# Two-block transformer kernel: layer norm sums full width in two banks, mean taken off the tiles during the variance, scale by Ln and Exp, pilot of two tiles

## The chip, the cores and the metric

One core of one Trainium2 chip. The metric is the device time of one execution in microseconds (us). The profile is of one execution, and its times count from its first instruction. The engines are PE (TensorE; PEld is its weight load), DVE (VectorE), ACT (ScalarE), POOL (GpSimd) and SP (SyncE, which here issues the weight loads).

## The reference

Two blocks on x of shape 512 tokens x 1024 features, all in fp32. The first block ends in a layer norm, and the second, a pre-norm transformer of two layers, starts from its output:

```
o = concat(out_a, out_b) @ w_out
x = layer_norm(ALPHA * x + gate * o, ln_g, ln_b, 1e-5)      # mean, then mean of (x - mean)^2
# second block, layer 0 (MLA), layer 1 (HGRN2):
a = rms_norm(h, g0);  proj = a @ mla_w_in;  c_q, c_kv, k_r = split(proj)
q = rms_norm(c_q) @ w_uq;  kv = rms_norm(c_kv) @ w_ukv;  ... attention ...
h = h + rms_norm(m, g1);  a = rms_norm(h, g2);  h = h + rms_norm(relu(a @ w1)^2 @ w2, g3)
```

The angles of the rotary embedding (positions x inv_freq, then sine and cosine) are computed on the core too.

## The kernel before

Activations lie feature-major: eight tiles of 128 features x 512 tokens (M is the mixer's output, XH the residual, "mix_out" and "resid" in the profile). A matmul job multiplies one 128-column slice of a weight matrix by the eight tiles. To keep fp32 precision each operand is split into a high and a low fp32r part, and a job is 24 matmuls of 512 columns (high x high, high x low, low x high) into one PSUM bank. All jobs of the kernel are numbered. O0 + k are the eight of w_out, I0 + j the six of the MLA input and H0 - 1 its last one, 64 columns wide.

For each job SP loads the raw weights into one of two slots, ACT converts them to the high part (`high`, w_high, L1378), POOL subtracts to get the low part (`low`, w_low, L523), and PE waits for it. Jobs alternate between banks 0 and 1, so PE also waits until DVE has emptied a bank (the semaphores free["o"], free["mi"]). `high(c)` waits for job c - 2, as its slot must be free. Every engine's order is written out by hand: what stands ahead in an engine's queue runs first.

The stretch of the change:
- `out_tile(k)` on DVE empties job O0 + k: M[k] = bank * gate + XH[k], and frees the bank.
- The layer norm needs mean and variance over the features, that is over partitions and tiles. DVE adds the tiles into sum_sq (SQA). After four tiles (PILOT) PE sums SQA over partitions with a matrix of ones (the pilot mean, bank 2), ACT copies it to R2, and `centre(k)` on DVE subtracts it from each tile, so that the squares stay small. ACT squares the centred tiles into ln_squares (LNSQ), and DVE adds these up in sum_sq_kv (SQK).
- PE then sums SQA, SQK and tiles 6 and 7 and their squares into columns, one token per partition (`columns`, L1081). DVE and ACT make mean and 1/deviation in 4 columns, DVE spreads them on two diagonals, PE turns these into full-width banks 3 and 4 (L1096), and DVE makes M[k] * bank 3 - bank 4 for each tile.
- `pre_norm_of_mla` on ACT writes act_high (L1564) and LNSQ (L1566) from each finished tile, POOL makes act_low (L531), and PE's `two_jobs(I0)` starts tile by tile (L744).
- Then ACT squares, DVE adds (L366), PE sums (`norm_sum`, L1105), ACT takes the square root (`deviation`, L1557) and DVE its reciprocal (`inverse`, L2264), giving R1, which scales each latent (`latent(j)`). The kv latents get their own R3 the same way. `deviation` and `inverse` are used a third time ahead of the HGRN heads. In each HGRN head ACT takes Ln and then Exp of the same tile (L1840, L1842).
- The angles of the rotary embedding are made on DVE (L2198 to L2213) between out_tile(3) and out_tile(4), while ACT takes their sine behind R1.

DVE's helpers are `tt` (L1882, two tensors) and `stt` (L1885, tensor, scalar, tensor), so many of its operations have these lines.

## Time and profile before

| | |
|---|---|
| time, median of 3 runs | 1844.92 us (1842.28 to 1846.31) |
| the profiled execution: its time, its span | 1843.03 us, 1841.3 us |
| PE, DVE, ACT, POOL busy | 92%, 47%, 40%, 35% |
| the eight output jobs on PE | 437.6 to 476.3 us |
| first tile's act_high on ACT | 494.4 us |
| first matmul of the MLA input | 497.5 us |

A row of the timeline gives start, duration, engine, line, operation, output<-inputs, shape and count, and in brackets the engine's idle time before it and what ended it. Where several operations are merged the duration is from the first one's start to the last one's end. The granted clock is a share of TensorE's full speed: 1.0 is 2.4 GHz, 0.5 is 1.2 GHz.

### The profile page before, as it was taken

What the parts mean: (1) busy time and instruction counts of PE and PEld (TensorE: products, weight loads), DVE (VectorE), ACT (ScalarE), POOL (GpSimd) and SP (SyncE); (2) the same over time, 40 slices, a digit from 0 to 9 for tenths busy, and PEclk for the clock granted to TensorE, in tenths of its full rate; (3) what the DMA queues carried; (4) which work ended last, traced back from release to release, by engine and by line L of the source; (5) the groups of instructions that cost most, each with busy time, mean ns of one, the idle gap of its engine ahead of it and who ended that gap; (6) DMA issues with size and microseconds to landing.
All of it is one profiled execution on the core that took longest, in us unless ns stands there. A gap on an engine that the chain in (4) does not pass through costs nothing.

```text
span 1841.3 us, 29716 instructions
## 1 busy us (share of the span) xinstructions
PE 1688.9 (92%) x10630; PEld 1372.6 (75%) x10630; DVE 863.0 (47%) x1472; ACT 737.0 (40%) x1152; POOL 651.9 (35%) x385
## 2 busy tenths in 40 slices
PE   3998978778789999999999999899998999999997
PEld 3786667755566677878888888688886878888886
DVE  4628867656684443452212125656664551212125
ACT  1322333322454543632323236576764542323232
POOL 4345310002432113554444445233332543444441
PEclk9999989998799999999999999899999999999997
DMA  9422210002111112232333332122221233333331
GB/s 306 153 84 71 63 47 3 3 2 60 46 43 38 34 46 75 64 97 82 101 91 103 91 103 61 55 69 68 68 68 54 73 92 82 101 92 102 91 100 61
DMA packets 250859, 140.18 MB, mean 76 GB/s; under 512 B 10089, under 2 KB 242624, under 8 KB 250768
## 3 DMA queue, kind: packets, MB, share of 16 engines
q1 hardware_dynamic: 249072, 135.03, 25.5%
q10 hardware_dynamic: 688, 2.23, 0.3%
q0 software_dynamic: 1008, 1.66, 0.3%
q8 instruction: 63, 1.03, 0.2%
q14 instruction: 28, 0.23, 0.0%
HBM read 136.80 MB, written 2.10 MB: 75 GB/s over the span
## 4 chain that ended last, share of the span: by engine, by line
issue 50%; PE 17%; POOL 14%; DVE 9%; DVEq 3%; ACT 3%; DMA 2%; POOLq 1%; ACTq 0%; SPq 0%
POOL w_low L523 13%; PE bank L688 7%; PE bank L867 3%; PE bank L978 2%; DVE bank L1882 1%; DMA w_ada_piece<-in_w_ada 1%; DVEq L2316 1%; DVEq L1889 1%; PE bank L744 1%; DVE v_centred L1882 1%; DVE mix_out L1882 1%; PE bank L881 1%; POOL w_low_z L538 0%; PE bank L1081 0%; DMA w_raw<-in_mlp_w 0%
## 5 line engine op out<-in xcount | busy, mean ns | idle before, releaser
L523 POOL TENSOR_TENSOR w_low<-w_raw,w_high 128x1024 fp32r<-128x1024 f32 (+1 forms) x232 | 527.8, 2275 | 1051.4 <-ACT w_high L1378 1051.1
L688 PE MATMUL bank<-act_high,w_high 128*128 128x512 f32 x992 | 396.2, 399 | 10.5 <-POOL w_low L523 8.0
L688 PE MATMUL bank<-act_high,w_low 128*128 128x512 f32 x992 | 387.3, 390 | 0.0
L688 PE MATMUL bank<-act_low,w_high 128*128 128x512 f32 x992 | 387.0, 390 | 0.0
L1378 ACT ACTIVATE w_high<-w_raw 128x1024 fp32r<-128x1024 f32 (+1 forms) x232 | 225.3, 971 | 287.3 <-PE bank L688 264.4
L688 PEld LDWEIGHTS bank<-act_high,w_high 128*128 128x128 f32 x992 | 186.2, 188 | 63.2 <-POOL w_low L523 12.5
L688 PEld LDWEIGHTS bank<-act_high,w_low 128*128 128x128 f32 x992 | 186.0, 188 | 40.5
L688 PEld LDWEIGHTS bank<-act_low,w_high 128*128 128x128 f32 x992 | 186.4, 188 | 39.1 <-issue 2.4
L688 PE MATMUL bank<-hid_high,w_high 128*128 128x512 f32 x488 | 192.1, 394 | 4.1 <-DVE mix_out L2536 3.8
L688 PE MATMUL bank<-hid_high,w_low 128*128 128x512 f32 x488 | 191.2, 392 | 0.0
L688 PE MATMUL bank<-hid_low,w_high 128*128 128x512 f32 x488 | 191.1, 392 | 0.0
L1882 DVE TENSOR_TENSOR tmp<-tmp 128x512 f32<-128x512 f32 x64 | 48.2, 753 | 220.7 <-ACTq L1773 220.7
L1882 DVE TENSOR_TENSOR mix_out<-bank,mix_out 128x512 f32 (+2 forms) x54 | 34.2, 632 | 192.7 <-PE bank L688 184.5
L688 PEld LDWEIGHTS bank<-hid_high,w_high 128*128 128x128 f32 x488 | 92.3, 189 | 25.9 <-DVE mix_out L2536 4.6
L1771 ACT ACTIVATE tmp<-bank 128x512 f32<-128x512 f32 x64 | 38.2, 597 | 180.9 <-PE bank L688 179.8
L688 PEld LDWEIGHTS bank<-hid_high,w_low 128*128 128x128 f32 x488 | 92.3, 189 | 19.6
L688 PEld LDWEIGHTS bank<-hid_low,w_high 128*128 128x128 f32 x488 | 92.5, 190 | 19.0
L1882 DVE TENSOR_TENSOR hid_low<-tmp,hid_high 128x512 f32 x64 | 50.2, 784 | 20.3 <-ACT hid_high L1775 17.2
L1775 ACT ACTIVATE hid_high<-tmp 128x512 f32 (+1 forms) x64 | 40.5, 633 | 15.5 <-issue 15.5
L547 POOL TENSOR_TENSOR act_low<-mix_out,act_high 128x256 fp32r<-128x256 f32 x48 | 34.3, 735 | 27.7 <-ACT act_high L1708 27.5
L714 PE MATMUL bank<-ones,tmp 128*128 128x1 f32 x96 | 18.0, 317 | 28.3 <-DVEq L1908 28.3
L1885 DVE SCALAR_TENSOR_TENSOR hg_state<-hg_state,hg_decay,bank 128x128 f32<-128x128 f32 x112 | 39.0, 348 | 10.4
(536 smaller groups left out, 2915.7 us busy)
## 6 DMA issues: line engine op xcount, KB each, us to landing
w_raw<-in_mlp_w SPq DMA_DIRECT2D x128, 512.0 KB, 4.1
w_raw<-in_hgrn_w_in SPq DMA_DIRECT2D x32, 512.0 KB, 4.1
w_raw<-in_w_in SPq DMA_DIRECT2D x29, 512.0 KB, 4.0
w_ada_piece<-in_w_ada SPq DMA_DIRECT2D x6, 2048.0 KB, 13.5
w_raw<-in_w_out SPq DMA_DIRECT2D x8, 512.0 KB, 4.0
w_raw<-in_mla_w_o SPq DMA_DIRECT2D x8, 512.0 KB, 4.0
w_raw<-in_hgrn_w_o SPq DMA_DIRECT2D x8, 512.0 KB, 4.0
w_raw<-in_mla_w_in SPq DMA_DIRECT2D x6, 512.0 KB, 3.9
```

Source lines behind the costliest of these rows:

```text
L523: gp.tensor_tensor(WL[:, c0 % 2, 0:kt, 0:m], WR[:, c0 % 2, 0:kt, 0:m], WH[:, c0 % 2, 0:kt, 0:m].bitcast(F32), ALU.subtract).then_inc(w_lo, 1)
L547: gp.tensor_tensor(AL[:, k, HALF[h]], M[:, k, HALF[h]], AH[:, k, HALF[h]].bitcast(F32), ALU.subtract).then_inc(act_lo, 1)
L688: mm = pe.matmul(bank[0:m, :], w[:, s, k, 0:m], a[:, k0 + k, :], start=(k == 0 and w is WH and a is hi), stop=(k == kt - 1 and w is WL))
L744: mm = pe.matmul(PB[c % 2][:, :], w[:, c % 2, k, :], a[:, k, :], start=(k == 0 and w is WH and a is hi), stop=(k == KT - 1 and w is WL))
L867: mm = pe.matmul(hs(h, bank), left[p:p + HB, j, :], right[p:p + HB, j, :], start=True, stop=True)
L881: pe.matmul(PB[1 + h % 2][:, j * P:(j + 1) * P], BK[p:p + HB, j, :], AR[s1][p:p + HB, j, :], start=True, stop=True)
L978: mm = pe.matmul(bank[:, HALF[h]], w[:, k, :], a[:, k, HALF[h]], start=(k == 0 and w is wh and a is hi), stop=(k == KT - 1 and a is last))
L1378: act.activation(WH[:, c0 % 2, 0:kt, 0:m], WR[:, c0 % 2, 0:kt, 0:m], ACT.Copy).then_inc(w_hi, 1)
L1771: act.activation(TMP[2 + s][:, :], (bank if bank is not None else PB[(j0 + s) % 2])[:, :], ACT.Relu)
L1775: act.activation(HH[:, bass.ds(i * 2 + s, 1), :], TMP[2 + s][:, :].rearrange("p (a t) -> p a t", a=1), ACT.Square)\
L1882: return dve.tensor_tensor(out_, a, b, op)
L1885: return dve.scalar_tensor_tensor(out=out_, in0=a, scalar=sc, in1=b, op0=op0, op1=op1)
```

## The change

- The pilot is of two tiles. After it DVE takes the pilot mean, straight from bank 2, off M[0..2] and off the residual tiles XH[3..7]. So out_tile(3..7) give centred tiles at once, and ACT's copy of the mean goes. Of these eight subtractions two (XH[3], XH[4]) stand ahead of out_tile(3), the other six between out_tile(3) and the angles.
- DVE adds all of tiles 0 to 6 and their squares. PE sums SQA and SQK with the matrix of ones at full width into banks 3 and 4, and accumulates tile 7 and its square on top.
- DVE makes mean squared and variance at full width. ACT makes Ln and Exp(-0.5 x) of it into bank 5. Meanwhile DVE takes the mean (bank 3) off tiles 0 to 3. Then each tile is multiplied by bank 5, and the mean is taken off tile k + 4 in turn.
- `deviation` and `inverse` become `rstd_of` (Ln and Exp on ACT, written straight to R1 or R3) and a wait, in all three places.
- On ACT the sine moves ahead of the square of tile 4, and the high part of O7's weights ahead of all but four of the squares.

The diff, with unchanged lines left out:

```diff
--- before.py
+++ after.py
@@ -208,7 +208,6 @@
 OTOK = at("out_tok", 88, [P, TT, D])
 DIAG = at("rstd_diag", 134, [P, TT, P])
-DIAGM = at("mean_diag", 132, [P, TT, P])
 DEVC = at("dev_cols", 140.5, [P, TT])
 RSTDC = at("rstd_cols", 140.53125, [P, TT])
 PREC = at("pre_cols", 140.5625, [P, TT])
@@ -368,8 +367,7 @@
     engine.sem_inc(nm_dve, 1)
 SBANK = (2, 3, 7, 2)
-PILOT = KT // 2
-LNM, LNV, LNR, LNMR = (SMALL[:, 44 + TT * n:44 + TT * (n + 1)] for n in range(4))
+PILOT = 2
 GLN, BLN = MOD[:, 0:KT], MOD[:, KT:2 * KT]
 LAT_BANK = (PB[1], PB[0], PB[4], PB[5], PB[1], PB[0])
 LAT = [QL + k for k in range(KVL)] + list(range(QL))
@@ -1075,26 +1073,13 @@
     for k in range(PILOT + 1, KT):
         job(O0 + k, 0, free["o"], k + 1)
-    def columns(c, src, first=False, last=False):
-
-        for t in range(TT):
-            mm = pe.matmul(PB[5][:, c + t:c + t + 1], src[:, t * P:(t + 1) * P], ONES[:, 0:1],
-                           start=first and t == 0, stop=last and t == TT - 1)
-        return mm
-
     pe.wait_ge(ln_dve, 2)
-    columns(0, SQA, first=True)
-    columns(TT, SQK)
-    for k in (KT - 2, KT - 1):
-        pe.wait_ge(ln_sub, k + 1)
-        columns(0, M[:, k, :])
-        pe.wait_ge(ln_sq, k + 1)
-        mm = columns(TT, LNSQ[:, k, :], last=k == KT - 1)
-    mm.then_inc(ln_pe, 1)
-    for n, diag in ((3, DIAG), (4, DIAGM)):
-        pe.wait_ge(ln_dve, n + 1)
-        pe.matmul(PB[n][:, :], ONES[:, :], diag[:, :, :].rearrange("p t s -> p (t s)"), start=True, stop=True)\
-            .then_inc(ln_pe, 1)
+    pe.matmul(PB[3][:, :], ONES[:, :], SQA[:, :], start=True, stop=False)
+    pe.matmul(PB[4][:, :], ONES[:, :], SQK[:, :], start=True, stop=False)
+    pe.wait_ge(free["o"], KT + 2)
+    pe.matmul(PB[3][:, :], ONES[:, :], M[:, KT - 1, :], start=False, stop=True).then_inc(ln_pe, 1)
+    pe.wait_ge(ln_sq, KT)
+    pe.matmul(PB[4][:, :], ONES[:, :], LNSQ[:, KT - 1, :], start=False, stop=True).then_inc(ln_pe, 1)
     norms = [0]
@@ -1519,25 +1504,32 @@
     act.dma_start(FC[:, :], inv_freq).then_inc(pos_loaded, 16)
     def square_centred(k):
-        act.wait_ge(ln_sub, k + 1)
+        if k <= PILOT:
+            act.wait_ge(ln_sub, k + 1)
+        else:
+            act.wait_ge(free["o"], k + 3)
         act.activation(LNSQ[:, k, :], M[:, k, :], ACT.Square).then_inc(ln_sq, 1)
-    for k in range(2, KT - 1):
+    for k in range(2, 6):
         high(O0 + k)
-    act.wait_ge(ln_pe, 1)
-    act.activation(R2[:, :], PB[2][:, :], ACT.Copy, scale=1.0 / (PILOT * P)).then_inc(ln_act, 1)
     for k in range(3):
         square_centred(k)
-    high(O0 + KT - 1)
-    for k in range(3, 6):
-        square_centred(k)
+    high(O0 + 6)
+    square_centred(3)
+    high(O0 + 7)
+    act.wait_ge(rp_ang, 1)
+    act.activation(SIN[:, :], ANG[:, :], ACT.Sin).then_inc(rp_sin, 1)
+    square_centred(4)
+    act.activation(SMALL[:, 44:44 + TT], CST[:, 3:4].broadcast_to([P, TT]), ACT.Ln)
+    square_centred(5)
     high(I0)
-    square_centred(KT - 2)
+    square_centred(6)
     high(I0 + 1)
-    act.activation(LNV, CST[:, 3:4].broadcast_to([P, TT]), ACT.Sqrt)
     square_centred(KT - 1)
     act.wait_ge(ln_dve, 3)
-    act.activation(LNV, LNV, ACT.Sqrt, bias=CST[:, 0:1]).then_inc(ln_act, 1)
+    act.activation(R2[:, :], R2[:, :], ACT.Ln, bias=CST[:, 0:1])
+    act.drain()
+    act.activation(PB[5][:, :], R2[:, :], ACT.Exp, scale=-0.5).then_inc(ln_act, 1)
     norms, squares = [0], [0]
@@ -1550,12 +1542,13 @@
             act.wait_ge(nm_sq, squares[0])
             act.activation(TMP[(squares[0] - 1) % 2][:, :], src[:, k, :], ACT.Square).then_inc(nm_act, 1)
-    def deviation(n, eps=3, dst=R2, bank=2):
+    def rstd_of(n, dst, bank, eps=3):
         norms[0] += 1
         act.wait_ge(nm_pe, norms[0])
-        act.activation(dst[:, :], PB[bank][:, :], ACT.Sqrt, scale=1.0 / n, bias=CST[:, eps:eps + 1])\
-            .then_inc(nm_dev, 1)
+        act.activation(dst[:, :], PB[bank][:, :], ACT.Ln, scale=1.0 / n, bias=CST[:, eps:eps + 1])
+        act.drain()
+        act.activation(dst[:, :], dst[:, :], ACT.Exp, scale=-0.5).then_inc(nm_dev, 1)
     def pre_norm_of_mla():
@@ -1572,10 +1565,8 @@
     pre_norm_of_mla()
     high(I0 + 2)
-    deviation(D)
-
-    act.wait_ge(rp_ang, 1)
-    act.activation(SIN[:, :], ANG[:, :], ACT.Sin).then_inc(rp_sin, 1)
+    rstd_of(D, R1, 2)
+
     def latent_high(k):
         g = col("q_norm", k) if k < QL else col("kv_norm", k - QL)
@@ -1590,7 +1581,7 @@
     square_latent(1)
     high(I0 + 4)
     square_latent(2)
-    deviation(KVL * P, dst=R3, bank=3)
+    rstd_of(KVL * P, R3, 3)
     high(I0 + 5)
     square_latent(3)
     for k in range(KVL):
@@ -1795,7 +1786,7 @@
     mlp(0, F0)
     high(G0 + 4)
-    deviation(D)
+    rstd_of(D, R1, 2)
     def hgrn(n, o, second=False):
@@ -2176,8 +2167,13 @@
             .then_inc(free["o"], 1)
         dve.drain()
-    def centre(k):
-        tt(M[:, k, :], M[:, k, :], R2[:, :], SUB).then_inc(ln_sub, 1)
+    def centred(tile):
+
+        return stt(tile, PB[2][:, :], -1.0 / (PILOT * P), tile, MUL, ADD)
+
+    def add_centred(k):
+
+        tt(SQA[:, :], M[:, 0, :] if k == 1 else SQA[:, :], M[:, k, :], ADD)
     def add_square(k):
@@ -2189,11 +2185,18 @@
     tt(BLN, col("ln_b", 0, KT), gain(0, 0, 0, KT), MUL)
     for k in range(PILOT):
         out_tile(k)
-        if k == 0:
-            dve.tensor_copy(SQA[:, :], M[:, k, :])
-        else:
-            tt(SQA[:, :], SQA[:, :], M[:, k, :], ADD)
+    tt(SQA[:, :], M[:, 0, :], M[:, 1, :], ADD)
     after(ln_dve)
+    out_tile(2)
+    dve.wait_ge(ln_pe, 1)
+    for k in (3, 4):
+        centred(XH[:, k, :])
+    dve.drain()
+    out_tile(3)
+    for k in range(3):
+        centred(M[:, k, :]).then_inc(ln_sub, 1)
+    for k in range(5, KT):
+        centred(XH[:, k, :])
     dve.wait_ge(pos_loaded, 32)
     dve.tensor_copy(ANG[:, :], PIX[:, :])
     dve.drain()
@@ -2212,45 +2215,43 @@
         dve.drain()
     dve.tensor_scalar(ANG[:, :], ANG[:, :], -3.1415925, 3.1415925, ALU.max, ALU.min)
     after(rp_ang)
-    out_tile(PILOT)
+    out_tile(4)
+    for k in (1, 2):
+        add_centred(k)
+        add_square(k)
+    out_tile(5)
+    for k in (3, 4):
+        add_centred(k)
+        add_square(k)
+    add_centred(5)
+    out_tile(6)
+    add_centred(6)
+    add_square(5)
+    add_square(6)
+    dve.sem_inc(ln_dve, 1)
+    out_tile(7)
+    dve.sem_inc(free["mi"], 2)
+    dve.wait_ge(ln_pe, 2)
+
+    def less_mean(k):
+
+        stt(M[:, k, :], PB[3][:, :], -1.0 / D, M[:, k, :], MUL, ADD)
+
+    dve.tensor_scalar(R1[:, :], PB[3][:, :], 1.0 / D, None, MUL)
+    dve.drain()
+    stt(R1[:, :], PB[3][:, :], 1.0 / D, R1[:, :], MUL, MUL)
+    dve.drain()
+    dve.wait_ge(ln_pe, 3)
+    stt(R2[:, :], PB[4][:, :], 1.0 / D, R1[:, :], MUL, SUB)
+    after(ln_dve)
+    for k in range(4):
+        less_mean(k)
+    dve.drain()
     dve.wait_ge(ln_act, 1)
-    for k in range(3):
-        centre(k)
-    out_tile(PILOT + 1)
-    for k in range(3, PILOT + 2):
-        centre(k)
-    dve.drain()
-    tt(SQA[:, :], M[:, PILOT, :], M[:, PILOT + 1, :], ADD)
-    add_square(1)
-    add_square(2)
-    out_tile(PILOT + 2)
-    centre(PILOT + 2)
-    for k in range(3, PILOT + 2):
-        add_square(k)
-    dve.sem_inc(ln_dve, 1)
-    out_tile(PILOT + 3)
-    centre(PILOT + 3)
-    dve.wait_ge(ln_pe, 2)
-    dve.tensor_scalar(LNM, PB[5][:, 0:TT], 1.0 / D, None, MUL)
-    dve.drain()
-    stt(LNR, LNM, -1.0, LNM, MUL, MUL)
-    dve.drain()
-    stt(LNV, PB[5][:, TT:2 * TT], 1.0 / D, LNR, MUL, ADD)
-    after(ln_dve)
-    dve.wait_ge(ln_act, 2)
-    dve.reciprocal(LNR, LNV)
-    dve.drain()
-    tt(LNMR, LNM, LNR, MUL)
-    tt(DIAG[:, :, :], bc1(IDENT[:, :], TT), bc(LNR, P), MUL).then_inc(ln_dve, 1)
-    dve.drain()
-    tt(DIAGM[:, :, :], bc1(IDENT[:, :], TT), bc(LNMR, P), MUL).then_inc(ln_dve, 1)
-    dve.sem_inc(free["mi"], 2)
-    dve.wait_ge(ln_pe, 4)
-    for k in range(KT + 1):
-        if k < KT:
-            tt(M[:, k, :], M[:, k, :], PB[3][:, :], MUL)
-        if k:
-            tt(M[:, k - 1, :], M[:, k - 1, :], PB[4][:, :], SUB).then_inc(resid_ready, 1)
+    for k in range(KT):
+        tt(M[:, k, :], M[:, k, :], PB[5][:, :], MUL).then_inc(resid_ready, 1)
+        if k + 4 < KT:
+            less_mean(k + 4)
         dve.drain()
     def residual(k):
@@ -2258,11 +2259,9 @@
     squares, devs = [0], [0]
-    def inverse(dst, src=R2):
+    def rstd_ready():
         devs[0] += 1
         dve.wait_ge(nm_dev, devs[0])
-        dve.reciprocal(dst[:, :], src[:, :])
-        dve.drain()
     outs = [0]
@@ -2358,7 +2357,7 @@
     dve.sem_inc(nm_sq, 2)
     add_tile_squares(dve, 0, LNSQ)
-    inverse(R1)
+    rstd_ready()
     def latent_square(j):
@@ -2405,7 +2404,7 @@
     after(rp_ang)
     latent_square(2)
     latent(3)
-    inverse(R3, R3)
+    rstd_ready()
     for k in range(QL, QL + KVL):
         tt(CQ[:, k, :], CQ[:, k, :], R3[:, :], MUL)
         after(cq_hi)
@@ -2560,7 +2559,7 @@
     mlp(0, F0)
     add_tile_squares(dve, 2)
-    inverse(R1)
+    rstd_ready()
     dve.wait_ge(const_pool, 3)
     def hgrn(n, o, second=False):
```

## Rows read from the trace of the kernel before

**Rows 1.** The page, part 1: busy time and share of the span, by engine.
```profile
PE 1688.9 (92%) x10630; PEld 1372.6 (75%) x10630; DVE 863.0 (47%) x1472; ACT 737.0 (40%) x1152; POOL 651.9 (35%) x385
```

**Rows 2.** Busy time by stage: us, each engine's busy time, granted clock, DMA.
```profile
437.60:479.30 41.70, 39.32 (x175) 31.38 (x173) 28.72 (x34) 12.93 (x17) 20.33 (x10) 1.00 0.33 92
...
479.30:486.40 7.10, 7.08 (x40) 6.99 (x39) 1.59 (x1) 0.63 (x1) 1.04 (x1) 0.60 0.28 76
...
492.35:505.80 13.45, 7.45 (x21) 4.52 (x21) 10.37 (x16) 11.37 (x17) 9.01 (x7) 0.67 0.00 0
```

**Rows 3.** Timeline of PE, 458 to 498 us.
```profile
458.13 1.02 PE L1074 MATMUL bank<-sum_sq,ones 128*128 128x512 f32 x2
...
470.54 0.50 PE L688 MATMUL bank<-act_high,w_high 128*128 128x512 f32 x1 [0.43 <-POOL w_low L523]
...
478.21 1.05 PE L1081 MATMUL bank<-ones,sum_sq 128*128 128x1 f32 x8 [1.95 <-DVEq L2186]
...
490.40 1.91 PE L1096 MATMUL bank<-mean_diag,ones 128*128 128x512 f32 x2
...
497.45 0.76 PE L744 MATMUL bank<-act_high,w_high 128*128 128x512 f32 x1 [5.13 <-POOL act_low L531]
```

**Rows 4.** Timeline of DVE, 454 to 504 us.
```profile
454.54 2.42 DVE L2198 CAST angle<-positions_sb 64x512 f32<-64x512 int32 x1
...
458.09 0.42 DVE L2204 CAST sin<-angle_k 64x512 f32<-64x512 int32 x1
...
458.59 4.24 DVE L1885 SCALAR_TENSOR_TENSOR angle<-sin,angle 64x512 f32<-64x512 f32 x3
...
463.45 0.75 DVE L1885 SCALAR_TENSOR_TENSOR mix_out<-bank,mod,resid 128x512 f32<-128x512 f32 x1
...
473.26 0.75 DVE L1885 SCALAR_TENSOR_TENSOR mix_out<-bank,mod,resid 128x512 f32<-128x512 f32 x1
...
474.11 1.89 DVE L1882 TENSOR_TENSOR mix_out<-mix_out,rstd_b 128x512 f32<-128x512 f32 x1
...
492.35 11.09 DVE L1882 TENSOR_TENSOR mix_out<-mix_out,bank 128x512 f32<-128x512 f32 x16 [3.09 <-PE bank L1096]
```

**Rows 5.** Timeline of POOL, 459 to 476 us.
```profile
459.52 2.76 POOL L523 TENSOR_TENSOR w_low<-w_raw,w_high 128x1024 fp32r<-128x1024 f32 x1 [2.85 <-ACT w_high L1378]
...
472.73 2.71 POOL L523 TENSOR_TENSOR w_low<-w_raw,w_high 128x1024 fp32r<-128x1024 f32 x1 [1.55 <-ACT w_high L1378]
```

**Rows 6.** Timeline of ACT, DVE and PE, from the first normed tile to 543 us.
```profile
494.43 0.81 ACT L1564 ACTIVATE act_high<-mix_out,mod 128x512 fp32r<-128x512 f32 x1 [7.01 <-DVE mix_out L1882]
...
513.82 0.69 ACT L1557 ACTIVATE rstd_b<-bank,consts 128x512 f32<-128x512 f32 x1 [1.39 <-PE bank L1105]
...
514.54 3.35 DVE L2264 RECIPROCAL rstd_a<-rstd_b 128x512 f32<-128x512 f32 x1 [1.97 <-ACT rstd_b L1557]
...
517.97 1.50 DVE L1882 TENSOR_TENSOR latents<-bank,rstd_a 128x512 f32<-128x512 f32 x2
...
523.38 1.12 PE L1105 MATMUL bank<-sum_sq_kv,ones 128*128 128x512 f32 x2 [2.71 <-DVEq L2372]
...
542.50 0.42 PE L688 MATMUL bank<-act_high,w_high 128*64 128x512 f32 x1 [1.64 <-DVEq L2380]
```

**Rows 7.** Instructions of lines 1840 and 1842: duration min/median/max, first and last start.
```profile
L1840 ACT ACTIVATE hg_out_dev<-bank,consts x8: 688/688/690, 1197.3 to 1400.1; 128x512 f32<-128x512 f32 x8
...
L1842 ACT ACT_TABLE_LOAD  x8: 1283/1283/1283, 1198.0 to 1400.9; - x8
...
L1842 ACT ACTIVATE hg_out_dev<-hg_out_dev x8: 630/632/632, 1199.3 to 1402.2; 128x512 f32<-128x512 f32 x8
```

**Rows 8.** Two gaps of PE: busy time of windows, and PE's timeline.
```profile
520.60:523.40 2.80, 0.09 (x2) 0.03 (x1) 2.42 (x1) 1.22 (x2) 2.80 (x2) 1.00 0.00 0
...
1155.65 1.24 PE L1105 MATMUL bank<-sum_sq,ones 128*128 128x512 f32 x2 [4.02 <-DVEq L367]
...
1157.00:1159.00 2.00, 2.00 (x6) 1.52 (x6) 1.35 (x1) 0.62 (x1) 0.00 (x0) 0.50 0.03 9
```

## The prediction

> **What bounds the kernel now.** I read the page first: TensorE is busy 92% of the span [rows 1], so what can be won lies in its gaps. The change touches the layer norm of the first block and what follows it, so next I read the busy time by stage [rows 2]. While the eight output jobs run (437.6 to 479.3) PE is nearly full at the full clock. Then come 7.1 us in which it is "busy" only with matmuls one column wide, then a silence, then 13.45 us in which it works half the time at a mean clock of 0.67.
>
> TensorE's own order of time [rows 3] gives the pieces. The pilot sum sits between jobs O4 and O5 (458.13, 1.02 us for its two halves). O7 starts at 470.54 after 0.43 of waiting for its low weights. The dense work ends at 478.21 - 1.95 = 476.3. The column sums follow, and a spread matmul at the low clock takes 1.91. The first matmul of the MLA input comes at 497.45. So 21.2 us lie between dense work and dense work. What ends the wait is a single chain: columns, small VectorE steps, two spreads, the first pair of tile operations at 492.35 on VectorE [rows 4], ScalarE's act_high at 494.43 [rows 6], its second copy, GpSimd's low part, PE. A us gained ahead of 494.43 is a us of the kernel.
>
> From 470.1 (470.54 less its wait) back to 458.13 lie two jobs and the pilot: with 0.9 for the pilot a job takes 5.5.
>
> **Part 1, the pilot after two tiles.** The same two matmuls, now behind O2: O3 to O5 end as before or 0.9 later, no cost by itself. But VectorE's order changes. Before, the angle chain (L2198 to L2213) stood behind out_tile(3) and one add, 454.54 to 463.45 [rows 4]. Now out_tile(3) waits for O3 at 453.7 (458.1 - 5.5, the pilot's 0.9, some 0.2 until the last matmul is out), and six subtractions of the pilot mean stand ahead of the chain: 453.7 + 0.75 + 6 x 0.69 = 458.6 (0.69 is 11.09/16, same tile size, one input in a bank). The chain took 8.9, of which about 4 is waiting: its first cast took 2.42 where the cast at 458.09 took 0.42, and three operations of 0.68 took 4.24. Both waits end with a weight subtraction on GpSimd (459.52 + 2.76 = 462.3) [rows 5]. Operations on two SBUF tiles do this repeatedly (474.11 took 1.89, GpSimd was busy until 475.44), while one with a bank as input, at 473.26 inside the same GpSimd operation, took its usual 0.75. Now the chain meets only one such subtraction: 458.6 + 4.9 + 2.0 to 2.7 = 465.5 to 466.2. out_tile(4) comes behind it and frees O6's bank at about 466.5; O6 could have begun at 464.6 (470.1 - 5.5). **PE loses 1.9**. ScalarE's w_high for O7 no longer stands behind three squares, its low part is ready by 468.5 (464.6, a conversion of about 1, a subtraction of 2.8), and the 0.43 ahead of O7 goes. Dense work ends at 476.3 + 1.9 - 0.4 = 477.8.
>
> **Part 2, the sums of tiles 1 to 6 on VectorE.** Behind out_tile(4) four adds of 0.69 meet O7's weight subtraction and start when it ends at 468.4: 471.2, and out_tile(5) ends at 471.9. Then come three adds of tiles and two of squares, after out_tile(6) three more. GpSimd's subtraction for I0 begins about 473.7 (ScalarE converts when O6 ends at 472.1) and holds VectorE until 476.3; out_tile(6) is done at 478.4. The last three adds start at 478.5, 479.1 and 479.9. ScalarE needs a square (0.63, as the same tile in [rows 7]) and a conversion of twice the size (about 1.1) behind out_tile(6), so GpSimd locks again only at 480.2, just behind the last add's start. Sums ready: **480.6**; out_tile(7), with a bank as input, 481.4. If the last add misses by 0.3, it waits 2.7 more.
>
> **Part 3, full width instead of columns.** Four sums over 512 columns. At the full clock one is 0.9, at the low clock 1.9 [rows 3]. Which clock? Window 479.3 to 486.4 has a mean of 0.60: 1.4 us at 1.0 and the rest at 0.5, so it fell at 480.7, 4.4 us after dense work ended, though the columns kept PE busy. A gap of 2.8 (520.6 to 523.4) left it at 1.0, one of 4.02 was followed by 0.50 [rows 8]. Here the gap is 477.8 to 480.6, and 477.8 + 4.4 = 482.2. I take two sums at full clock (482.4) and two at the low one: 484.3 and 486.2. Bounds: all four low, 488.2; all four full, 484.2.
>
> VectorE then needs mean 0.69, mean squared 0.75 (beside PE's last sum) and the variance 0.75: 487.0. ScalarE's Ln and Exp are not in this stretch before. The nearest rows are hgrn's pair, same size: Ln 0.69, a table load of 1.28, Exp 0.63 [rows 7], together 2.6: 489.7. Beside them VectorE takes the mean off four tiles, 2.8: 489.8. Then one multiplication of 0.69 and the first tile is ready at 490.6 where it was 494.43: **3.8 earlier**. Removed with it: seven small VectorE steps, the ScalarE square root, both diagonals, both spreads. Behind it VectorE has two operations a tile as before (16 in 11.09), ScalarE still two conversions a tile, GpSimd as before: PE's first matmul moves with it, to 493.6.
>
> The Trainium skill (ScalarE: Activation LUTs, "Table sets: the hidden batching unit") says that one set holds both ln and exp, so that the pair needs one load. The rows of hgrn show a load ahead of each Exp, so this program does not use that. With one load the sum would be -8.3, against -6.9 by the rows.
>
> The same page ("What ACT_TABLE_LOAD costs") adds a drain of about 1.38 to each switch, which speaks against the change. The trace's Exp follows its 1.28 load at once (1198.0 to 1199.3). With that drain in both places the sum would be about -4.2.
>
> **Part 4, R1 without the reciprocal.** Before: ScalarE's root at 513.82, reciprocal 3.35 at 514.54, first use 517.97, so 4.15 [rows 6]. Now 2.7 (its first load runs while ScalarE idles). The next thing on PE is the sum of the kv latents, for which it waited 2.71 at 523.38; its chain (two latents, two squares, an add that waits out a GpSimd subtraction) starts with R1. **1.45 earlier**. The sine leaves this place for the output jobs, where ScalarE idles.
>
> **Part 5, R3 likewise.** VectorE loses another 3.35, the same operation, ahead of latent(4), for which PE waited 1.64 at 542.50. ScalarE's longer R3 (3.9 with both loads) ends before the latent in front of it. That wait goes: **1.64**. What could be late next is the w_low of that job, which follows ScalarE's latent conversions; those come earlier too.
>
> **Part 6, R1 ahead of hgrn.** The reciprocal goes again, but by the program ScalarE stands next at the weights of G0 + 5, which wait for PE's job G0 + 3 and not for R1, and PE is in that job then. I take nothing (at most the 1.45 of part 4). Everything later shifts as a block.
>
> **Sum.** -3.8 - 1.45 - 1.64 = -6.9. The profiled execution took 1843.03 (span 1841.3, 1.7 around it), which becomes 1836.1. The median of before is 1844.92, 1.9 above that execution, and gives **1838.0**.
>
> **Rivals.**
> - *The clock holds.* All sums at full clock: last sum at 484.2, variance at 485.6, and four means and a product behind it give the first tile 1.5 earlier. Total -8.4, 1836.5. For it: the gap of 2.8 that left the clock up. Against: the fall 4.4 us after dense work. 0.13.
> - *No load ahead of Exp.* ScalarE is 1.28 shorter in both places. At the norm four means on VectorE end as late, so 0.1; at R1 1.3. Total -8.3, 1836.6, and with the clock held 1835.1. Against: a load at all eight of hgrn's Exp [rows 7]. 0.03. The one-set rule of the Trainium skill (ScalarE: Activation LUTs) would bring this.
> - *A switch of tables costs twice its load*, because the engine empties first: 1.3 more in both places, -4.3, 1840.6. Against: the Exp that follows its load at once. 0.05. The drain that the Trainium skill gives on the same page would act like this.
> - *The sums are late.* The low clock from the first sum costs 2.0 less what VectorE overlaps, 1.8; a last add that meets GpSimd 2.8. Totals -5.1, -4.1, both -2.3: 1839.8 to 1842.6. For it: the margin of 0.3. 0.22.
> - *The gain behind the norm is covered.* The add waiting for GpSimd's subtraction, or ScalarE's conversions, set those two starts whatever the reciprocals do: only -3.8, 1841.1. 0.14.
> - *Slower: VectorE becomes the bound of the output jobs.* Place: its queue from 453.7 to 480.6, in which twelve adds of two SBUF tiles now stand among the evictions. Each that begins under one of GpSimd's four subtractions waits up to 2.6. I have counted three such waits, the angles' included. If the last add ends 7 us later than 480.6 the kernel is level; slower by 0.2% takes 10.6, four further whole waits, and gives 1848.6. Against it: there are only four subtractions in the stretch, and evictions are not held. 0.07.
> - My forecast: 0.36.
>
> **How the numbers follow.** A change of 0.2%, 3.7 us, is about what a measurement of this kernel can tell from none, so faster means under 1841.2. The forecast, the clock rival, both table rivals, half of "late" and half of "covered" lie there: 0.36 + 0.13 + 0.08 + 0.11 + 0.07 = 0.75. The other halves, 0.18, are within 0.2%. Slower: 0.07. The range reaches from both clock and table gains with 0.6 for the runs' own spread (1834.5) to the late sums with all their costs (1843). Where all stays on the forecast's path: 1836.5 to 1839.5.
>
> **What would show it.** O6 starts near 466.5 after a wait for VectorE of about 2, O7 without a wait; the two sums begin near 480.6; the clock there tells between forecast and its first rival; a table load ahead of each Exp; act_high near 490.6 and PE near 493.6; R1 ready 2.7 after its sum; no wait ahead of the 64-wide job. I am wrong if the last add sits under a GpSimd subtraction, if O6 or O7 wait longer than 2, or if PE still waits 2.7 for the latents' sum and 1.6 for the 64-wide job.

## The result and the profile after

The changed kernel takes 1835.64 us (median of 8 runs, 1827.38 to 1838.92), the kernel before 1845.59 beside it (8 runs, 1841.88 to 1852.15). The ratio is 0.9932 [0.9909, 0.9954]: faster by 0.7%. On the 1844.92 of the prediction that is 1832.4, 5.6 below the forecast and 2.1 below its range. The direction was forecast, the size was not. By the medians the difference is 10.0. Three of the eight executions of the changed kernel lie at 1827.4 to 1828.7 and five at 1835.5 to 1838.9; the profiled one is of the first three, 8.1 below the median. Three executions in the later measurements (two of the kernel before, one of a filled kernel) took 2151 to 9233 us and stand in no ratio.

The page's head and its first part, after:

```profile
span 1825.7 us, 29634 instructions
PE 1674.0 (92%) x10586; PEld 1360.2 (75%) x10586; DVE 856.4 (47%) x1468; ACT 748.7 (41%) x1162; POOL 651.3 (36%) x385
```

One thing must be known before two timelines are laid beside each other: they are shifted already above the change. out_tile(2), the last eviction that both programs reach with the same jobs of TensorE done, starts at 447.45 before and at 444.64 after. So 2.8 us come from nothing that was changed, and all comparisons below are of durations from that mark. They run to the square root of the query latents' norm (RQ), which ScalarE does last before the heads begin:

| stretch (us) | before | after | difference | forecast |
|---|---|---|---|---|
| out_tile(2) to out_tile(7) | 30.8 | 32.9 | +2.1 | +2.4 |
| out_tile(7) to first act_high | 16.2 | 10.3 | -5.9 | -6.2 |
| act_high to first latent | 23.5 | 22.1 | -1.4 | -1.45 |
| first latent to RQ | 32.5 | 30.7 | -1.8 | -1.64 |
| sum | 103.0 | 96.0 | **-7.0** | **-6.9** |

(Forecast, first line: the prediction's 481.4 is the end of out_tile(7), so its start is 480.65, against 478.25 before. The first two lines together were forecast at -3.8 and came to -3.8.)

The marks of this table, first of before, then of after:

```profile
447.45 0.75 DVE L1885 SCALAR_TENSOR_TENSOR mix_out<-bank,mod,resid 128x512 f32<-128x512 f32 x1 [4.15 <-PE bank L688]
...
478.25 0.75 DVE L1885 SCALAR_TENSOR_TENSOR mix_out<-bank,mod,resid 128x512 f32<-128x512 f32 x1
...
550.48 0.26 ACT L1612 ACTIVATE small<-bank,consts 128x4 f32<-128x4 f32 x1
```

```profile
444.64 0.75 DVE L1876 SCALAR_TENSOR_TENSOR mix_out<-bank,mod,resid 128x512 f32<-128x512 f32 x1 [4.13 <-PE bank L686]
...
509.93 1.51 DVE L1873 TENSOR_TENSOR latents<-bank,rstd_a 128x512 f32<-128x512 f32 x2 [3.95 <-ACT rstd_a L1551]
...
540.61 0.26 ACT L1603 ACTIVATE small<-bank,consts 128x4 f32<-128x4 f32 x1
```

TensorE's order of time after, against [rows 3] and the last lines of [rows 6] (128*64 is the 64-wide job):

```profile
463.23 0.47 PE L686 MATMUL bank<-act_high,w_high 128*128 128x512 f32 x1 [1.41 <-DVE mix_out L1876]
469.05 0.47 PE L686 MATMUL bank<-act_high,w_high 128*128 128x512 f32 x1
477.53 1.43 PE L1077 MATMUL bank<-sum_sq,ones 128*128 128x512 f32 x2 [2.77 <-DVEq L2182]
478.75 1.92 PE L1078 MATMUL bank<-sum_sq_kv,ones 128*128 128x512 f32 x2
480.45 1.61 PE L1080 MATMUL bank<-mix_out,ones 128*128 128x512 f32 x2
481.90 1.02 PE L1082 MATMUL bank<-ln_squares,ones 128*128 128x512 f32 x2
490.86 0.77 PE L742 MATMUL bank<-act_high,w_high 128*128 128x512 f32 x1 [7.94 <-POOL act_low L529]
515.38 1.12 PE L1090 MATMUL bank<-sum_sq_kv,ones 128*128 128x512 f32 x2 [1.33 <-DVEq L2371]
532.68 0.39 PE L686 MATMUL bank<-act_high,w_high 128*64 128x512 f32 x1
```

O6 (463.23) waits 1.41 for out_tile(4); 1.9 was forecast. O7 (469.05) has no wait, as forecast. The four sums take the place of columns and spreads, and 13.3 us lie between the first sum and the first dense matmul, where [rows 3] has 19.2 from the first column to 497.45. The wait for the kv latents' sum is 1.33 instead of 2.71, and the 64-wide job (532.68) starts without the wait of 1.64.

VectorE, against [rows 4] (the second number is the duration of the whole group):

```profile
455.43 0.41 DVE L2201 CAST angle<-positions_sb 64x512 f32<-64x512 int32 x1
457.45 4.25 DVE L1876 SCALAR_TENSOR_TENSOR angle<-sin,angle 64x512 f32<-64x512 f32 x3
462.33 0.75 DVE L1876 SCALAR_TENSOR_TENSOR mix_out<-bank,mod,resid 128x512 f32<-128x512 f32 x1
470.97 2.89 DVE L1873 TENSOR_TENSOR sum_sq_kv<-sum_sq_kv,ln_squares 128x512 f32<-128x512 f32 x1
475.99 1.45 DVE L1873 TENSOR_TENSOR sum_sq_kv<-sum_sq_kv,ln_squares 128x512 f32<-128x512 f32 x2
477.57 0.75 DVE L1876 SCALAR_TENSOR_TENSOR mix_out<-bank,mod,resid 128x512 f32<-128x512 f32 x1
482.11 0.69 DVE L2240 TENSOR_SCALAR rstd_a<-bank 128x512 f32<-128x512 f32 x1 [3.79 <-PE bank L1080]
484.48 2.48 DVE L1876 SCALAR_TENSOR_TENSOR mix_out<-bank,mix_out 128x512 f32<-128x512 f32 x4
487.12 0.69 DVE L1873 TENSOR_TENSOR mix_out<-mix_out,bank 128x512 f32<-128x512 f32 x1 [0.16 <-ACT bank L1532]
```

and GpSimd, against [rows 5]:

```profile
470.60 2.72 POOL L521 TENSOR_TENSOR w_low<-w_raw,w_high 128x1024 fp32r<-128x1024 f32 x1 [4.45 <-ACT w_high L1363]
476.98 2.68 POOL L521 TENSOR_TENSOR w_low<-w_raw,w_high 128x1024 fp32r<-128x1024 f32 x1 [3.66 <-ACT w_high L1363]
```

These two views belong together. The cast that took 2.42 before takes 0.41; one subtraction is met in the chain instead of two. The add at 470.97 takes 2.89 instead of 0.69 because GpSimd has been at work since 470.60; of the last two (from 475.99) the second begins at 476.75, 0.23 before the subtraction at 476.98, and is not held. That is the margin that "the sums are late" doubted, and it held. out_tile(7) at 477.57, inside the same subtraction, has a bank as input and takes its usual 0.75. At 487.12 VectorE has waited 0.16 for ScalarE, so the four means and the Ln, load, Exp of ScalarE end together, as forecast (489.8 and 489.7 there).

ScalarE, in the norm (against [rows 7]) and at R1 (against [rows 6]):

```profile
484.42 0.72 ACT L1530 ACTIVATE rstd_b<-rstd_b,consts 128x512 f32<-128x512 f32 x1 [5.43 <-DVEq L1880]
485.20 1.28 ACT L1532 ACT_TABLE_LOAD   x1
486.49 0.60 ACT L1532 ACTIVATE bank<-rstd_b 128x512 f32<-128x512 f32 x1
487.85 0.81 ACT L1557 ACTIVATE act_high<-mix_out,mod 128x512 fp32r<-128x512 f32 x1 [0.76 <-DVE mix_out L1873]
...
505.86 1.28 ACT L1549 ACT_TABLE_LOAD   x1
507.23 0.69 ACT L1549 ACTIVATE rstd_a<-bank,consts 128x512 f32<-128x512 f32 x1
507.97 1.28 ACT L1551 ACT_TABLE_LOAD   x1
509.26 0.63 ACT L1551 ACTIVATE rstd_a<-rstd_a 128x512 f32<-128x512 f32 x1
```

A load of 1.28 stands ahead of each Exp, and the Exp starts as soon as it ends. Both table rivals fall with this line.

The clock, by windows after (us; then busy time and instructions of PE, PEld, DVE, ACT, POOL; granted clock; DMA share; GB/s):

```profile
477.50:483.00 5.50, 5.40 (x8) 2.03 (x8) 1.56 (x3) 0.63 (x1) 2.16 (x1) 0.69 0.37 95
540.60:548.60 8.00, 7.31 (x30) 4.79 (x30) 5.12 (x10) 2.23 (x6) 1.49 (x2) 1.00 0.17 49
548.60:565.00 16.40, 15.40 (x77) 10.24 (x77) 7.20 (x23) 7.48 (x18) 2.91 (x4) 1.00 0.15 41
749.00:759.00 10.00, 9.49 (x62) 9.03 (x63) 4.34 (x13) 2.98 (x8) 3.53 (x6) 0.83 0.14 41
759.00:1099.00 340.00, 336.77 (x1555) 279.65 (x1554) 92.47 (x130) 117.91 (x159) 158.91 (x77) 1.00 0.33 94
```

The sums run partly at 2.4 GHz and partly at 1.2 (0.69 in the mean; 1.92 for the second, 1.02 for the fourth). They take 5.4 in all, where the forecast had 5.6 and the rival "the clock holds" 3.6. The order was not the forecast one: the clock fell during the first sum and was full again for the fourth, where two full ones and then two low ones had been forecast. So the stretch of the change did what the prediction said, and its row sums to -7.0. The profiled span is 15.6 shorter all the same. The other 8.6 are 2.8 above the change and 5.8 below it, nearly all in code that is the same (the one changed place there is hgrn's R1). The windows of before at the place of the last two above, and one inside the second, show what they are made of:

```profile
759.00:769.00 10.00, 9.49 (x50) 8.96 (x50) 3.07 (x9) 1.53 (x5) 3.11 (x5) 0.66 0.12 35
769.00:1109.00 340.00, 336.82 (x1542) 279.12 (x1541) 93.31 (x132) 116.83 (x158) 157.27 (x76) 0.99 0.33 93
818.00:828.00 10.00, 8.11 (x29) 6.22 (x28) 3.45 (x5) 1.06 (x1) 2.36 (x1) 0.83 0.37 105
```

At the start of the first MLP the clock is 0.66 over 10 us before and 0.83 after: PE works as long (9.49) but gets through 50 matmuls instead of 62. Some 60 us further on, before has a second low stretch (0.83 over 818 to 828) and after has none (1.00 over 805 to 815). The whole MLP takes 350.9 before and 348.4 after, the second one 351.0 and 348.4. For every stretch I add up (1 - granted clock) over windows of 2 us and call it the time lost to the low clock. At the first MLP that is 3.6 before and 0.8 after, at the second 4.0 and 0.9. Over the span it is about 71 and 58.

### The profile page after: what moved, and what is told of

The parts are those of the page before. It is cut to its first block, busy times and chain, and to the rows that moved or that the text cites. A ratio compares the mean times of both kernels' runs of the same rounds, so it can differ in the third digit from the quotient of the medians.

```text
span 1825.7 us, 29634 instructions
## 1 busy us (share of the span) xinstructions
PE 1674.0 (92%) x10586; PEld 1360.2 (75%) x10586; DVE 856.4 (47%) x1468; ACT 748.7 (41%) x1162; POOL 651.3 (36%) x385
## 3 DMA queue, kind: packets, MB, share of 16 engines
q0 software_dynamic: 1008, 1.66, 0.3%
q8 instruction: 62, 1.02, 0.2%
## 4 chain that ended last, share of the span: by engine, by line
issue 50%; PE 18%; POOL 14%; DVE 9%; DVEq 4%; ACT 3%; DMA 2%; POOLq 1%; ACTq 0%; SPq 0%
POOL w_low L521 13%; PE bank L686 8%; PE bank L865 3%; PE bank L976 2%; DVE bank L1873 2%; DMA w_ada_piece<-in_w_ada 1%; DVEq L2315 1%; DVEq L1880 1%; DVE sum_sq L1873 1%; PE bank L742 1%; DVE v_centred L1873 1%; PE bank L879 1%; DMA w_raw<-in_mlp_w 0%; DVE tmp L1873 0%; DVE tmp L1876 0%
## 5 line engine op out<-in xcount | busy, mean ns | idle before, releaser
L686 PE MATMUL bank<-act_high,w_high 128*128 128x512 f32 x992 | 396.5, 400 | 10.2 <-POOL w_low L521 7.7
L742 PE MATMUL bank<-act_high,w_high 128*128 128x512 f32 x64 | 29.9, 467 | 16.1 <-POOL act_low L529 8.7
L1411 ACT ACTIVATE p_shift<-bank 128x512 f32<-128x512 f32 x17 | 10.2, 599 | 83.5 <-PE bank L686 83.5
```

What stands on the lines that cost most here:

```text
L686: mm = pe.matmul(bank[0:m, :], w[:, s, k, 0:m], a[:, k0 + k, :], start=(k == 0 and w is WH and a is hi), stop=(k == kt - 1 and w is WL))
L742: mm = pe.matmul(PB[c % 2][:, :], w[:, c % 2, k, :], a[:, k, :], start=(k == 0 and w is WH and a is hi), stop=(k == KT - 1 and w is WL))
```

## Experiments

The question is whether these 2.8 and 5.8 us belong to the change. One theory says that the kernel has won its 7 us of path and that the rest is the clock, which falls or not at each short gap of PE depending on the moment at which the gap comes. The rival says that the rest is earned too, through a mechanism that the prediction missed. The kernels were measured in four series, and those of one series share their runs of before: the first four, then e5 to e8, then e9 to e12, then e13 to e16 (medians of before 1843.95, 1844.45, 1844.66 and 1844.70, 23 to 35 runs each).

### Both kernels once more

No edit. The changed kernel as it is:

> The changed kernel once more, unchanged. Path theory: 7 us of the difference come from the norm and the two reciprocals and are there in every execution; the other 5 to 8 us come from how often TensorE's clock is at its low level in stages that the change does not touch, and vary by execution: this profile's span lies anywhere from 1825 to 1837, and where it is longer than 1825.7 the extra time lies in stretches at granted clock 0.5, in steps of about 1.7 us. Rival (the change itself does more than 7): the span is within 2 us of 1825.7 and the stages after the MLA input show the same low stretches as in the changed kernel's first profile.

The kernel before as it is:

> The kernel of before once more, unchanged. Path theory: ratio 1.000 within its interval, and this profile differs from the first one by up to 8 us, all of it in stretches at the low clock. Rival: it repeats 1841 to 1843 with the same low stretches.

The changed kernel: 1830.31, ratio 0.9934 [0.9913, 0.9956], span 1823.5, just outside what either theory asked for, path 96.0 again, both MLPs 348.2 and 347.5. Before: 1845.54, 1.0006 [0.9987, 1.0025], path 102.9, MLPs 351.0 and 351.0; but out_tile(2) comes at 450.1, where the first profile has 447.45. So the path repeats within 0.1, the upstream part differs by 2.7 between executions of one program, and so far the shorter MLPs go with the changed kernel.

### The two halves alone

Scales without a reciprocal, in the kernel before:

```
-            deviation(D)          # ACT: Sqrt, at three places
+            rstd_of(D, R1, 2)     # ACT: Ln, Exp
-            inverse(R1)           # DVE: reciprocal
+            rstd_ready()          # DVE: waits only
```

> The kernel of before with only the three pairs of root and reciprocal replaced by Ln and Exp on ScalarE. Prediction's steps: R1 ready 1.45 earlier, the wait of 1.64 ahead of the 64-wide job gone, nothing at hgrn: 3.1 us less (ratio 0.9983) apart from the clock. Rival (hgrn's start or the latents gain more): 5 us or more less. Rival (covered by GpSimd's subtractions): no change, PE still waits 2.7 and 1.6.

The opposite: the changed kernel with Sqrt and reciprocal back at these three places, so that only the norm is new.

> The changed kernel with root and reciprocal put back in the three places (R1, R3, hgrn's R1), so only the layer norm's part of the change is left. Prediction's steps: 3.8 us less than before (ratio 0.9979). Rival (the norm's part carries the surplus): 8 us or more less.

The scales alone: 1840.39, 0.9986 [0.9966, 1.0006], path 101.0 (-2.0). The first latent gains 1.4, the stretch behind it 0.8 instead of 1.6, although the wait ahead of the 64-wide job is gone there too. Two rows point at the sine, the first from ScalarE, the second from TensorE:

```profile
515.05 0.63 ACT L1579 ACTIVATE sin<-angle 64x512 f32<-64x512 f32 x1
...
520.24 1.13 PE L1105 MATMUL bank<-sum_sq_kv,ones 128*128 128x512 f32 x2 [2.35 <-DVEq L2371]
```

The sine and its table load of 1.28 still stand on ScalarE between R1 and the first square of a latent, which starts 1.85 behind R1 instead of 0.80. The kv latents' sum comes 6.5 after R1 instead of 5.5, and TensorE waits 2.35 for it instead of 1.33.

The norm alone: 1845.61, 1.0012 [0.9993, 1.0031], path 98.8 (-4.2). The paths add up to -6.2 of -7.0. The totals do not: -2.6 and +2.2 against the -10 to -12.5 of both together. The norm is the larger half of the path, and by itself it shows nothing in the total. Its trace, of an execution 8.3 above the median, shows one place where the 4.2 can go: the heads of the MLA layer are 168.7 us long where every profile so far had 162.3 to 163.8, with 6.8 lost to the low clock. That is code far behind the norm and the same in both kernels.

### The same change, later by 0.7, 1.3, 2.0 and 3.3 us

If the moment decides, a plain delay must change the total by something else than its length. ScalarE makes one to five copies that nothing reads, ahead of the Ln of the norm, where the whole core waits for it:

```
             act.wait_ge(ln_dve, 3)
+            for _ in range(2):          # 1, 2, 3, 5
+                act.activation(PB[6][:, :], XH[:, 0, :], ACT.Copy)
+                act.drain()
```

Two copies:

> The changed kernel with two copies of a tile into an unused bank ahead of the norm's Ln on ScalarE (their result is used by nobody): a pure delay of about 1.4 us on the one chain that starts the MLA input. Additive theory (each us of this chain is a us of the kernel, clock losses elsewhere are unrelated): 1.4 us over the changed kernel. Clock theory (TensorE's low-clock stretches after this point depend on when the work comes): the difference to the changed kernel is clearly not 1.4; the time less what the low clock costs goes up by 1.4 while the part lost to the low clock moves by several us either way.

Five:

> The same with five copies, about 3.5 us of delay. Additive theory: 3.5 us over the changed kernel. Clock theory: not 3.5, and not in proportion to the run with two copies.

and in the next series one and three:

> The changed kernel with one idle copy, about 0.7 us, ahead of the norm's Ln. Additive theory: 0.7 us over the changed kernel (1835.5 from its 1834.8). Clock theory: anywhere between the changed kernel and the run with two copies (1845), but the path to the MLA heads is 0.7 longer and the rest is time at granted clock 0.5.

> The same with three copies, about 2.1 us. Additive theory: 1837. Clock theory: between the run with two copies (1845.0) and the one with five (1835.9), not on the line through the changed kernel.

The same copies in the kernel before, ahead of its Sqrt:

> The kernel of before with one idle copy, about 0.7 us, ahead of ScalarE's root in the norm. Additive theory: ratio 1.0004. Clock theory: the time less what the low clock costs rises by 0.7, and the part lost to the clock moves by several us either way.

> The same with two copies, about 1.4 us. Additive theory: ratio 1.0007. Clock theory: off that line by more than its interval in at least one of the four delayed kernels of before, possibly to under 1.

> The same with three copies, about 2.0 us. Additive theory: ratio 1.0011. Clock theory as for two.

> The same with five copies, about 3.3 us. Additive theory: ratio 1.0018. Clock theory as for two. Taken together: if the surplus of the change is only the moment at which its work comes, the mean of the five times of before (delay 0 to 3.3, each less its delay) lies about 7 us above the mean of the five times of the changed kernel with the same delays, and not 10 to 12.

The undelayed kernel was in the second series too:

> The changed kernel a third time, for the comparison on one chip. Both theories: a span between 1824 and 1838; the stretch from the third output tile to the MLA heads takes 96.0 us as in its two other profiles, and what differs between profiles is time at granted clock 0.5.

| delay on the path | changed kernel, us | ratio | kernel before, us | ratio |
|---|---|---|---|---|
| 0 | 1834.75 | 0.9945 [0.9922, 0.9969] | 1845.54 | 1.0006 [0.9987, 1.0025] |
| 0.7 | 1836.11 | 0.9957 [0.9937, 0.9977] | 1848.39 | 1.0013 [0.9994, 1.0032] |
| 1.3 | 1845.00 | 0.9995 [0.9974, 1.0016] | 1845.45 | 1.0011 [0.9994, 1.0029] |
| 2.0 | 1838.40 | 0.9972 [0.9952, 0.9992] | 1847.36 | 1.0016 [0.9998, 1.0033] |
| 3.3 | 1835.85 | 0.9951 [0.9930, 0.9973] | 1845.71 | 1.0008 [0.9998, 1.0019] |

The delay is the growth of the stretch from out_tile(7) to act_high, 10.3, in the changed kernel: 11.0, 11.6, 12.3, 13.6. In the kernel before the same copies moved act_high by 0.6, 1.0, 3.7 and 2.8, and RQ by 2.2, 2.6, 3.7 and 5.6, so the delay itself is only roughly the same there.

A delay of 1.3 costs the changed kernel 10 us by the medians (9 by the ratios), one of 3.3 costs 1. Nothing earned by a shorter path behaves like this. It is this one delay that leaves the additive line clearly. Counted from the 0.9945 of the second series the other three of the changed kernel stay within their intervals (counted from 0.9937, the mean of its three measurements, the one of 2.0 is just outside), and none of the four of the kernel before does, where the clock theory had asked for at least one. Nor do the shorter MLPs stay with the changed kernel: the first one takes 350.7, 350.6 and 351.1 with delays of 0.7, 1.3 and 2.0, and 348.3 with 3.3; and the second took 347.5 in the kernel before with nothing but the scales changed. The trace of the delay by 1.3 shows where they go. Windows, from the last sum of the latents on:

```profile
545.50:553.50 8.00, 8.00 (x28) 5.77 (x29) 3.83 (x8) 1.57 (x4) 0.87 (x2) 0.79 0.12 22
553.50:570.00 16.50, 14.84 (x45) 9.95 (x45) 5.49 (x16) 5.38 (x11) 2.61 (x3) 0.59 0.14 37
```

and, in its order of time on TensorE, the one wait in there:

```profile
555.83 0.30 PE L692 MATMUL bank<-w_high,latents_high 128*128 128x128 f32 x1 [1.66 <-DVEq L1883]
```

PE waits 1.66 us for VectorE ahead of the first head's values. The changed kernel has the same wait in the same place:

```profile
549.60 0.30 PE L692 MATMUL bank<-w_high,latents_high 128*128 128x128 f32 x1 [1.68 <-DVEq L1880]
```

There the clock is 1.00 in all 16.4 us around it; here it is 0.59 over 16.5 us, with 45 matmuls done instead of 77. The heads take 170.1 instead of 162.3, 8.5 of it lost to the low clock.

Sixteen of the eighteen profiles have this wait, 1.66 to 1.68 long; the two filled kernels below do not. The clock falls behind it in three: here, with the norm alone, and in the kernel before with three copies (0.58 over 16.4 us, heads 168.6). What the clock was ahead of the wait does not decide. Over the 8 us behind RQ it was 1.00 with the norm alone, and 0.79 with a delay of 2.0, as here. The norm alone, then the delay of 2.0:

```profile
559.20:575.60 16.40, 15.36 (x48) 10.65 (x49) 4.22 (x15) 4.68 (x11) 2.12 (x2) 0.58 0.09 24
```

```profile
555.90:572.00 16.10, 14.44 (x70) 9.18 (x69) 7.33 (x22) 7.71 (x17) 3.38 (x4) 1.00 0.20 55
```

The averages over the moments are worth more than any one total. With each delay taken off its ratio (0.0004, 0.0007, 0.0011, 0.0018), and the repeats of the undelayed kernels averaged, the changed kernel has 0.9937, 0.9953, 0.9988, 0.9961 and 0.9933, in the mean 0.9954; the kernel before 1.0003, 1.0009, 1.0004, 1.0005 and 0.9990, in the mean 1.0002. The difference is 0.0048, 8.8 us, with a standard error of about 2 from the spread of the five. The path gives 7.0. Expected had been about 7 against 10 to 12: 8.8 lies nearer to the 7, but its error does not exclude 10.

### The gap filled

The strongest test takes the wait away from PE without moving anything behind it. Seven matmuls that nobody reads, into a bank that is free there, ahead of the first head's values, in the kernel with the delay of 1.3:

```
+            def fill(bank, src, n):
+                for _ in range(n):
+                    pe.matmul(bank[:, :], src[:, 0, 0:P], src[:, 0, :], start=True, stop=True)
...
                 if n is not None:
+                    if o is None:
+                        fill(PB[7], CQH, 7)
                     job(H0 + 3, n * 4, h_r, n + 1, ...)
```

> The slow one of the delayed kernels (two copies, 1845.0) with seven matmuls whose result nobody reads, in PE's 1.7 us wait ahead of the first head's values. If the idle gap there, at a bad moment, is what sends TensorE to its low clock for some 14 us (8.6 us lost in that kernel's profile), the stage of the MLA heads goes back from 170 to about 162 us and the kernel to about 1837. Rival (the length of that stage has another cause, or the fall was already decided ahead of the gap): 1843 or more, and the stage stays at 168 to 170.

1834.81, 0.9946 [0.9926, 0.9966]: 10.2 less than the same kernel without them, 9 by the ratios. Its seven executions in the ratio lie at 1828.5 to 1837.0, the twelve without the filling at 1842.05 to 1850.3. PE's order of time and the windows of the same stretch:

```profile
550.44 1.75 PE L1079 MATMUL bank<-latents_high 128*128 128x512 f32 x7
552.27 0.30 PE L692 MATMUL bank<-w_high,latents_high 128*128 128x128 f32 x1
```

```profile
541.90:549.90 8.00, 8.00 (x28) 5.66 (x29) 3.79 (x9) 1.60 (x5) 0.82 (x2) 0.79 0.11 28
549.90:566.00 16.10, 16.02 (x77) 10.50 (x76) 7.34 (x22) 7.59 (x17) 3.50 (x4) 1.00 0.19 52
```

The first window is the same as without them (28 matmuls, 0.79). In the second the clock is 1.00 where it was 0.59, and 77 matmuls are done, seven of them the added ones. Nothing on the path is earlier. The heads take 163.7, of which 1.7 are lost. This one place is 6.3 of the 9.9 between the two spans (1842.7 and 1832.8); 3.6 more lie above out_tile(2), where nothing differs. So this filled profile also meets the wait at another moment. That the filling and not the moment kept its clock up rests on the executions, which do not overlap, and not on the one trace.

The changed kernel filled at three places, ten such matmuls ahead of the norm's sums, seven ahead of the first head's values and fourteen ahead of the sum before hgrn:

```
+            fill(PB[6], AH, 10)
             pe.wait_ge(ln_dve, 2)
...
-                    after_head(G0 - KT, f_dn[0], LAST_DN, hook=norm_sum)
+                    after_head(G0 - KT, f_dn[0], LAST_DN, hook=lambda: (fill(PB[5], AH, 14), norm_sum()))
```

> The changed kernel with unread matmuls in three gaps of PE: 10 ahead of the norm's sums (wait of 2.8), 7 ahead of the first head's values (1.7), 14 ahead of the sum at the start of hgrn (4.0). Clock theory: four sums of the norm at full clock, up to 1.3 us on the path, and the low stretch of 3.4 us after the hgrn gap gone (1.7); 2 to 3 us below the changed kernel, and fewer of its slow executions. Rival: the added matmuls delay what stands behind them, no gain or up to 2 slower.

1830.42, 0.9922 [0.9896, 0.9947]. Its ratio is the lowest here. It lies 4.3 under the 1834.75 of the changed kernel in the second series, but level with the 1830.31 of the first, and the intervals overlap: a gain in the total is not shown. PE around the norm's sums:

```profile
477.96 2.43 PE L1079 MATMUL bank<-act_high 128*128 128x512 f32 x10
480.88 1.13 PE L1083 MATMUL bank<-sum_sq,ones 128*128 128x512 f32 x2 [0.49 <-DVEq L2190]
...
483.56 1.02 PE L1088 MATMUL bank<-ln_squares,ones 128*128 128x512 f32 x2
```

All four sums take their 1.0 at 2.4 GHz and out_tile(7) to act_high shrinks from 10.3 to 8.6: 1.7 for sums at full clock throughout, against the 1.5 of the rival "the clock holds". The stretch from the first MLP to hgrn takes 29.1 instead of 30.3 to 32.4.

### The angles behind out_tile(4)

The one cost of the change, PE's wait ahead of O6, seems easy to save: out_tile(4) goes ahead of the angle chain.

```
                 centred(XH[:, k, :])
+            out_tile(4)
             dve.wait_ge(pos_loaded, 32)
...
             after(rp_ang)
-            out_tile(4)
```

> The changed kernel with out_tile(4) ahead of the angle chain on VectorE instead of behind it, all else equal. By the trace PE waits 1.41 us for out_tile(4) ahead of O6. Path theory: that wait goes, the sums begin up to 1.4 earlier, 1.4 us less than the changed kernel apart from the clock. Rival: the angle chain then stands ahead of the first adds and meets two of GpSimd's subtractions, out_tile(5) is late instead, and nothing is won on the path.

1837.94, 0.9968 [0.9950, 0.9986], beside 1834.75 of the changed kernel in the same series. out_tile(2) to out_tile(7) takes 33.9 instead of 32.9 and the whole path 96.9 instead of 96.0. O6 is free at once, but the chain and four adds now stand ahead of out_tile(5), and TensorE waits 2.75 for it ahead of O7, where it had waited 1.41 ahead of O6. That is the rival's course. Nothing is won.

## Why the prediction was right and where it was wrong

**The path was right.** The sum of -6.9 stands against -7.0 in all three profiles of the changed kernel.
- Part 1: O6 waited 1.41 (1.9 forecast), O7's 0.43 went.
- Part 2: out_tile(7) ended at 478.3 + 2.8 of shift = 481.1 where 481.4 was forecast. The last add ended at 477.4 + 2.8 = 480.2 (480.6). "The sums are late" did not come about; its margin, forecast at 0.3, was 0.23 and held in all three profiles of the undelayed kernel.
- Part 3: first act_high at 487.85 + 2.81 = 490.66, forecast 490.6. Within it the sums ran at 0.69 of the clock, and the variance and the Exp took what hgrn's rows gave. That the sums' total fits is in part luck: the clock fell earlier than forecast, and came back, which the prediction did not have. The trace settled two figures that the prediction had weighed: the Trainium skill (ScalarE: Activation LUTs, "Table sets: the hidden batching unit" and "What ACT_TABLE_LOAD costs") would have one load for ln and exp, or a drain of about 1.38 at each switch. In this program a load stands between Ln and Exp, and 0.01 us lies between the load's end and the Exp. The measurement decides for the rows of hgrn, on which the sum stood.
- Part 4: 1.4 of the 1.45. PE's wait fell by 1.38, from 2.71 to 1.33. But the prediction put this gain down to the reciprocal alone. With the scales alone R1 was as early and PE still waited 2.35; the rows put the other 1.0 down to the sine, which the change moved away from this place.
- Part 5: the wait of 1.64 ahead of the 64-wide job is gone, 1.8 on the path behind the first latent. With the scales alone 0.8 came there (PE's wait for the sum stayed at 2.35), with the norm alone 0.4 (its wait ahead of the 64-wide job stayed at 1.22).
- Part 6, first half: hgrn's R1 gave nothing that can be seen beside the clock: from the end of the first MLP to hgrn 31.5 before and 31.6 after in the first profiles.

"VectorE becomes the bound" and "the gain behind the norm is covered" fall with the same lines: VectorE waits 3.79 for PE at 482.11, and the path behind the norm is 3.2 shorter where 3.1 was forecast. With the scales alone it is 2.2 shorter: about 1 would have been covered if the sine had stayed.

**Wrong was one sentence: "Everything later shifts as a block" (Part 6).** And with it the range, which priced the clock only inside the norm. Behind the change the same code took 2.5 and 2.6 less in the two MLPs, because a stretch at 1.2 GHz at its start lasted some 3.4 us instead of 6.8, and one of 3.4 some 60 us later did not come. The direction was luck: with a delay of 1.3 the same mechanism gave back 8 us in the MLA heads, and the kernel would have measured at 1845.0, no faster than before. The term that was missing is one of either sign: plus 7 or 8, or minus 5 to 6, whichever moment the gaps fall into. For this change at a moment not known beforehand, -7 with these two sizes beside it makes some 1832 to 1846, not 1834.5 to 1843. That is an estimate from two profiles, made after the fact.

The bound of 0.2% for what can be told from no change was too small as well. Single runs of the changed kernel lie 11.5 apart (1827.38 to 1838.92), and out_tile(2), above the change, came at 443.9 to 452.4 in eighteen profiles (444.5 to 452.4 on one chip alone), and the time lost to the low clock ahead of it was 23.9 in the earliest and 35.8 in the latest.

The gain that belongs to the change is then 7.0 by the path and 8.8 (about 2 either way) by the averages over delays. The first measurement, 12.5 by its ratio and 10 by its medians, has another 1 to 5.5 in it that this change does not own. Open stays what makes the clock fall at one moment and not at another, why the part upstream differs between executions, and whether the 1.8 between 8.8 and 7.0 is real or within the error.

## What to carry to other kernels

A change of a few microseconds is judged by its own stretch, between two marks in the profile, before its total; the path repeated within 0.1 in three profiles whose spans differed by 6.5. If a total has to decide, run the changed kernel with three or four plain delays of a microsecond or less beside it: one that wins 10 and loses it at +1.3 has won something else. Where TensorE waits 1 to 3 us in an otherwise dense stretch, matmuls that nobody reads are a cheap trial. Here one such filling was worth 9 to 10 us in a version whose clock fell at that wait, 6 of it seen in the trace at that place. In a version whose clock did not fall there, three fillings gave 1.7 on the path and no gain in the total that can be told from none.
